# The expert stage's first buffer for high parts of a pair of weight slots, moved by 96 bytes

## The reference

```python
def moe_swiglu(t, router, w_gate, w_up, w_down):      # t: 256 x 1024, 8 experts of width 3584
    logits = (t @ router).astype(jnp.float32)
    top_logits, top_idx = lax.top_k(logits, TOP_K)    # TOP_K = 2
    gates = jax.nn.softmax(top_logits, axis=-1)
    combine = jnp.sum(jax.nn.one_hot(top_idx, N_EXPERTS, dtype=jnp.float32) * gates[..., None], axis=1)
    out = jnp.zeros_like(t)
    for e in range(N_EXPERTS):
        out = out + combine[:, e:e + 1].astype(t.dtype) * swiglu(t, w_gate[e], w_up[e], w_down[e])
    return out
```

## The kernel before, in words

| tensor | start | start % 128 |
|---|---|---|
| raw ring, `moe_pair_low0` to `2`, `split_ring` | 16512 and multiples of 8192 on | 0 |
| `operand_high`, `operand_low` | 73856, 82048 | 0 |
| `moe_down_high0` | 98432 | 0 |
| `moe_pair_high1`, and `late_high0` of other stages | 138976 | 96 |
| `late_high1` of other stages | 147168 | 96 |
| arena | 163200 | 0 |
| `hidden_high0` to `hidden_low1` | 185728 to 191872 | 0 |
| `moe_pair_high0` | 193920 | 0 |
| `moe_down_high1` | 210304 | 0 |
| `moe_down_low1`, and the raw slot of odd down steps | 218496 | 0 |

## Time and profile before

### The profile page before, as it was taken

The page is one execution under the profiler, slowest core; times in us unless marked ns, Lnnn a source line. Parts: engine busy times, 40 slices in busy tenths (PEclk is TensorE's granted clock), DMA queues, the critical chain, the costliest instruction groups (busy, mean ns, idle before and its releaser), DMA issues.

```text
span 1855.9 us, 28476 instructions
## 1 busy us (share of the span) xinstructions
PE 1805.4 (97%) x11353; PEld 1566.4 (84%) x11353; DVE 1410.5 (76%) x1579; ACT 1140.9 (61%) x1254; POOL 96.1 (5%) x117
## 2 busy tenths in 40 slices
PE   8989999999998999999999999999999999899997
PEld 8868999988887888888888888888888887889997
DVE  6766665563637889889898888898888887886674
ACT  6544533344436767677676676776766775765753
POOL 0042000010210000000000000000000000201010
PEclk9999999998998999999999999999999999999999
DMA  8100455543316989899898898998988988533431
GB/s 357 69 24 3 179 185 182 182 159 114 114 46 273 363 341 365 328 376 356 338 369 352 342 365 340 359 358 337 373 345 343 376 355 305 181 136 137 159 137 46
DMA packets 64210, 467.17 MB, mean 252 GB/s; under 512 B 7248, under 2 KB 7376, under 8 KB 7888
## 3 DMA queue, kind: packets, MB, share of 16 engines
q1 hardware_dynamic: 64080, 465.36, 64.5%
HBM read 464.28 MB, written 1.05 MB: 251 GB/s over the span
## 4 chain that ended last, share of the span: by engine, by line
PE 86%; DVE 7%; ACT 3%; DMA 2%; issue 2%; POOL 0%; SPq 0%; ACTq 0%; DVEq 0%; POOLq 0%
PE bank L573 84%; PE bank L583 2%; DMA weight_ring<-w_dram 2%; DVE split_ring L2211 1%; ACT arena L1601 1%; ACT split_ring L1601 0%; ACT late_high L1601 0%; DVE arena L2247 0%; ACT operand_high L1601 0%; DVE arena L2216 0%; DVE operand_low L2257 0%; DVE arena L2248 0%; ACT L1601 0%; POOL squares L3083 0%; DVE arena L2981 0%
## 5 line engine op out<-in xcount | busy, mean ns | idle before, releaser
L2827 DVE TENSOR_TENSOR moe_pair_low<-weight_ring,moe_pair_high 128x2048 fp32r<-128x2048 f32 x225 | 507.1, 2286 | 14.2 <-ACT moe_pair_high L1601 13.7
L1601 ACT ACTIVATE moe_pair_high<-weight_ring 128x2048 fp32r<-128x2048 f32 x225 | 427.1, 1918 | 36.8 <-DMA weight_ring<-w_dram 35.5
L573 PE MATMUL bank<-moe_pair_high,operand_high 128*128 128x512 f32 x896 | 354.5, 396 | 2.2 <-DVE operand_low L2834 2.2
L573 PE MATMUL bank<-moe_pair_high,operand_low 128*128 128x512 f32 x896 | 352.4, 393 | 0.0
L573 PE MATMUL bank<-operand_high,split_ring 128*128 128x256 f32 x1536 | 293.4, 286 | 3.2 <-ACT split_ring L1601 1.1
L1601 ACT ACTIVATE arena<-bank 128x256 f32<-128x256 f32 (+4 forms) x221 | 88.8, 423 | 300.8 <-PE bank L573 276.5
L573 PEld LDWEIGHTS bank<-operand_high,split_ring 128*128 128x128 f32 x1536 | 240.6, 192 | 7.3 <-issue 5.1
L573 PE MATMUL bank<-moe_pair_low,operand_high 128*128 128x512 f32 x896 | 223.4, 391 | 0.0
L573 PEld LDWEIGHTS bank<-moe_pair_high,operand_high 128*128 128x128 f32 x896 | 169.0, 189 | 39.4 <-issue 2.4
L573 PEld LDWEIGHTS bank<-moe_pair_high,operand_low 128*128 128x128 f32 x896 | 169.0, 189 | 36.5
L573 PEld LDWEIGHTS bank<-moe_pair_low,operand_high 128*128 128x128 f32 x896 | 168.1, 188 | 37.4
(11 more groups left out here) (315 smaller groups left out, 3061.4 us busy)
## 6 DMA issues: line engine op xcount, KB each, us to landing
weight_ring<-w_dram SPq DMA_DIRECT2D x381, 1024.0 KB, 6.9
arena<-w_dram SPq DMA_DIRECT2D x55, 1024.0 KB, 4.8
parameters<-param_dram SPq DMA_DIRECT2D x1, 2896.5 KB, 24.5
constants<-const_dram SPq DMA_DIRECT2D x1, 2836.0 KB, 17.6
hT<-x_dram SPq DMA_DIRECT2D x1, 1024.0 KB, 5.1
out_dram<-squares SPq DMA_DIRECT2D x4, 256.0 KB, 2.2
constants<-const_dram SPq DMA_DIRECT2D x1, 128.0 KB, 4.7
parameters<-param_dram SPq DMA_DIRECT2D x1, 54.5 KB, 4.7
```

Of the source, the lines that this page charges most:

```text
L573: return pe.matmul(out, lhsT, rhs, start=start, stop=stop, skip_group_check=True)
L1601: return act.activation(out, in_, f, **kw)
L2827: tt(low_, raw_, high_.bitcast(F32), ALU.subtract).then_inc(moe_split, 1)
```

## The change

The arena becomes 32 float32 (128 bytes) longer. In its division for the experts, 24 float32 (96 bytes) of gap go ahead of `moe_pair_high0` and 8 (32 bytes) behind it. `moe_pair_high0` so starts at 194016, which is 96 past a multiple of 128 (and 224 past one of 256, as 138976 is). Everything that lies behind it in the arena, `moe_down_high1` (210432), `moe_down_low1` and the raw slot of odd down steps (218624) and the attention stages' scratch, moves by 128 bytes and still starts at multiples of 128. What lies ahead of it stays. No instruction is added, removed or put elsewhere.

```diff
@@ -186,17 +186,19 @@
         tiny = sb("tiny", 192)
         zero16 = sb("zero16", P, BF16)
         passes_i = sb("expert_passes", 1, I32)
-        ARENA = 15872
+        ARENA = 15904
         with nc.sbuf_tensor("arena", [P, ARENA], F32) as arena:
             pass
 
 
         with ExitStack() as over:
-            over.enter_context(nc.sbuf_tensor("arena_start", [P, ARENA - 4 * SLOT - 4 * 512 - T], F32))
+            over.enter_context(nc.sbuf_tensor("arena_start", [P, ARENA - 4 * SLOT - 32 - 4 * 512 - T], F32))
             ohT = over.enter_context(nc.sbuf_tensor("onehot_turned", [P, T], F32R))
             hhi = [over.enter_context(nc.sbuf_tensor(f"hidden_high{i}", [P, 512], F32R)) for i in range(2)]
             hlo = [over.enter_context(nc.sbuf_tensor(f"hidden_low{i}", [P, 512], F32R)) for i in range(2)]
+            over.enter_context(nc.sbuf_tensor("gap_ahead_of_pair", [P, 24], F32))
             pair_high0 = over.enter_context(nc.sbuf_tensor("moe_pair_high0", [P, 2 * SLOT], F32R))
+            over.enter_context(nc.sbuf_tensor("gap_behind_pair", [P, 8], F32))
             down_high1 = over.enter_context(nc.sbuf_tensor("moe_down_high1", [P, SLOT], F32R))
             down_low.append(over.enter_context(nc.sbuf_tensor("moe_down_low1", [P, SLOT], F32R)))
         down_raw = [ring[:, 6 * SLOT:7 * SLOT], arena[:, ARENA - SLOT:ARENA]]
```

## The result

The changed kernel takes 1869.21 us (median of 5, 1866.56 to 1874.05) against 1859.04 (5 runs, 1858.14 to 1859.75): 10.2 us more, ratio 1.0061, 95% interval 1.0049 to 1.0073 (the two medians alone give 1.0055).

What follows compares the result with a forecast made beforehand. TensorE's expert-stage matmuls were taken to bound the kernel. Even steps added 7.1 + 0.8 = 7.9 us, with the last down step (at most 0.06) 8.0: 1859.04 + 8.0 = 1867.0 us, range 1863.0 to 1870.0.

Steps and rivals of the forecast that it cites:

- What bounds the kernel: Expert stage: TensorE is busy for whole steps, so time added to its matmuls is added to the run.
- the main term: Even expert steps take the odd steps' passes, 3.74 and 1.85 us, gaining 0.145 us per plain step; chance 0.76.
- that of no change: Rival, expert steps: PSUM bank or buffer region sets the beat, so the move does nothing, 1859.0 us; chance 0.10.
- the rule of the 16-byte lines: SBUF access: 0 and 96 are both multiples of 16, so the move would be free, 1859.0 us.
- that of the other engines' access (faster): Rival, odd expert steps: ScalarE's and VectorE's aligned access slows TensorE; the move gives 8.1 us less, 1850.9; chance 0.05.
- a part of the price: Rival, even expert steps: the `pair_low` pass finds the beat again or the region is kinder, 5.9 us, 1864.9; chance 0.09.
- The step that failed: Odd down passes: the 128-byte move of their buffers, still at multiples of 128, taken as 0.
- Its bound: Odd down passes: 0.007 us for each of 12 matmuls in 56 steps, 4.7 us either way, given little weight.
- The other term, that of the pair: Even steps' two passes with `pair_high[0]` at 96: 49 x 0.145 + 7 x 0.11 = 7.9 us more.
- What would show it: Changed kernel's windows: even steps 8.56 us like odd ones, passes 3.74 and 1.85, ScalarE's and VectorE's groups keeping their means.
- The expert of 125.01 us: Sign in the expert stage: one expert's window of 125.01 us takes some 126.0 in the changed kernel.

Runs made afterwards that it cites:

- run 3: Kernel before with `pair_high[1]` moved 160 bytes up, so both pair buffers start at multiples of 128: 1853.77 us against 1859.93, ratio 0.9966.
- run 9: Kernel before with `operand_high` and `operand_low` moved by 96 bytes and all behind them by 256: 1867.12 us against 1858.98, ratio 1.0048.
- run 7: Against the kernel before, pair unmoved and one gap of 32 float32 behind it, moving the rest by 128 bytes: 1862.68 us against 1858.22, ratio 1.0025.
- run 2: Changed kernel with `pair_high[0]` still at 96, all behind it moved by 256 bytes instead of 128: 1866.21 us against 1859.93, ratio 1.0032.
- runs 8: Against the kernel before, `pair_high[0]` moved by 32 bytes and all behind it by 256: 1866.22 us against 1858.22, ratio 1.0039.
- 11: Against the kernel before, `pair_high[0]` moved by 64 bytes and all behind it by 256: one execution of 1859.03 us, even first pass 3.68 us.
- 6: Against the kernel before, `pair_high[0]` moved by 128 bytes and all behind it by 256: 1865.07 us against 1858.22, ratio 1.0038.
- run 5: Kernel before with one 128-byte gap ahead of the first tensor, moving every tensor by 128: 1858.40 us against 1858.22, ratio 0.9997.

## Why the prediction came out as it did

*What bounds the kernel* held: the stage is TensorE's, and what was added to its matmuls was added to the run. VectorE's and ScalarE's idle time grew, and nothing became late.

*The direction and the main term.* Plain even steps lost their beat as the odd ones, with the odd ones' price: 3.75 and 1.85 us against the 3.74 and 1.85 forecast. Against the rivals: that of no change (the bank, or the rule of the 16-byte lines) fell with the result and with run 3, where both banks keep the beat; that of the other engines' access (faster) fell with the result; and a part of the price is not what happened in either pass of the changed kernel. That rival of the bank had been held against the earlier trace rows, but the row over `split_ring` there is eight loads merged into one and shows their total, no single distance; run 3 is what settles it. The Trainium skill's rule of 16-byte lines (Advanced Engine Details and Errata, SBUF Cachelines) has no room for prices between places that are all multiples of 32; 3.63, 3.72, 3.68, 3.74 and 3.72 us for distances of 0, 32, 64, 96 and 128 differ by up to 3%, and the measurement decides. The Trainium skill's statement that TensorE's port never waits for another engine (SBUF — State Buffer, SBUF: two separate sides) is not contradicted by any run: the first passes went from 3.63 to 3.74 us and back with the places of TensorE's own operands, in run 9 while both buffers of the pair stayed where they were within 256 bytes.

*The size.* The sum was 8.0 us; the stage shows 10.25 and the medians 10.2. The median of 1869.21 us lies just inside the range's end at 1870; the ratio put on 1859.04 is 1870.4, with an interval of 1868.1 to 1872.6, just past it. The step that failed is the one on `moe_down_high1` and `moe_down_low1`: "They stay at multiples of 128 [...] so this is taken as 0". It measured 4.1 us by itself (run 7) and 4.0 as the difference of the changed kernel and run 2. Its bound, 4.7 us either way, had held it, but I gave it little weight and left it out of the range's upper end; 1867.0 + 4.7 would have been 1871.7. What stood behind this was the picture that a multiple of 128 is the right place. The rows could not show better: everything aligned in the kernel before stood at 128 modulo 256 together with all the loaded weights, so a multiple of 128 and a distance of 0 modulo 256 were the same thing. I had noted that no row separated them, and still took 0 because the offsets "stay".

The other term, that of the pair, was 7.9 us and measured 6.2 (run 2). The first and second pass of the even step grew as forecast, but behind them the down passes of both kinds of step found the beat three matmuls sooner than in the kernel before, so that the even step grew by some 0.13 us and not 0.145, and the odd one shrank from 8.56 to 8.55. Summed over the stage from the starts of the steps, the even ones took 6.9 us more and the odd ones 0.7 less. Why they found it sooner stays open. The two errors had opposite signs, 4.1 too little and 1.7 too much; that the sum was only 2.2 us short is in part luck.

*What would show it* was right for the even steps and ScalarE's and VectorE's groups. The odd steps were to stay at 8.56; their 8.60 was the first sign of the missing term. The expert of 125.01 us was to take some 126.0 and took 126.33 from the start of step 39 to that of step 53.

## What to carry to other kernels

Look at the distance between the starts of single weight loads, not at a matmul's mean: where passes of the same shape come in two lengths, compare where their operands start. In split products like these, of 512 columns, give the moving operand the same place within 256 bytes as the loaded weights; a tensor of odd size among the allocations cost up to 3% of such a pass here (3.74 against 3.63 us), and moving one buffer moves all that are placed behind it. When rows don't separate two rules (a multiple of 128, or a distance of 0 modulo 256), the term that hangs on the choice belongs in the range in full.

## What the runs showed of the hardware

- A first pass of 16 matmuls (2 runs of 256 float32 each) takes 3.63 us at distance 0 modulo 256 bytes from the loaded weights, and 3.72, 3.68, 3.74, 3.72 at 32, 64, 96, 128 (runs 8, 11, 2 and the earlier trace rows, 6; these all with the down buffers in their place), and 3.74 at 160, with the weights moved (run 9).
- Only the distance matters: all tensors moved by 128 together change nothing (run 5, 974.95 us both), the weights alone moved by 96 shift the full price from the odd passes to the even ones (run 9). Distances that are odd and even multiples of 256 serve alike: the weights are at 73856, `pair_high[0]` 469 x 256 behind them, and `moe_down_high1` is 96 x 256 behind `hidden_high0` in the kernel before and 97 x 256 in run 2, with 8.56 and 8.55 us for the odd step.
- Lost beat outlives its cause: passes at distance 0 that follow one out of beat take 1.85 us instead of 1.81 for 8 matmuls and 3.68 instead of 3.63 for 16 (run 7). In run 9 a pass at distance 0 took 3.68 us behind a down pass at distance 0, with weights of another place loaded at the change-over. How the matmuls find it again, and what in the chip keeps it, no run here shows; that part stays open.
- Two profiled executions of one kernel differed by 8.9 us ahead of the experts, with 0.95 and 0.98 of granted clock there, and by 0.03 us in the stage with 1.00. For a change of some us in one stage, that stage's window told more than the timed medians.
